# Feed-forward gate and up products by seven block products instead of eight, with the four weight sums of a pair on GpSimd

## The chip, the cores and the metric

One core of one Trainium2 chip. The time is the device time of one execution in microseconds (us), the median of several runs; lower is better.

## The reference, cut to what matters

The model has 528 tokens (16 learned and 512 given), a width of 1024 and two layers. The first layer mixes tokens by attention, the second by a recurrence (RWKV-7), and each ends in a feed-forward part. The change touches that part alone, and there the first of the two products:

```python
def swiglu(h, w_in, w_out):                      # w_in 1024 x 5632, w_out 2816 x 1024
    gate, up = jnp.split(jnp.einsum('btd,df->btf', h, w_in), 2, axis=-1)
    return jnp.einsum('btf,fd->btd', jax.nn.silu(gate) * up, w_out)

for i in range(DEPTH):
    ...
    h = h + mix
    h = h + swiglu(rms_norm(h, ffn_norm[i]), w_ffn_in[i], w_ffn_out[i])
return rms_norm(h[:, N_META:], final_norm)
```

## The kernel before, in words

Everything lies transposed: features on the 128 partitions, tokens along the row. A **unit** is a weight tile that gives 128 output features: 8 blocks of 128 x 128 (1024 inputs) for gate, up and the projections, 11 blocks for half of the 2816 hidden features. All weights are f32 in memory and are cut into two fp32r parts, high and low, so that each block needs three matmuls: high by high, high by low, low by high.

A unit goes through four engines, with two buffers of each kind. SyncE's DMA queue loads the raw tile (`load_unit`, L126). ScalarE copies it to fp32r (`w_hi`, L130). VectorE subtracts that from the raw tile (`w_lo`, L134). TensorE multiplies (`unit_products`, L790, and `Mlp.part`, L1257). The order on every engine is written out by hand, and semaphores hold them together.

The feed-forward part is the class `Mlp`. It first does 8 units of the mixer's output projection, each with the residual sum (L965), the high and low part of the normed input without its 1/rms (L893, L949) and the running sum of squares (L935); two small matmuls give the mean square (L1219) and ScalarE its inverse root by Ln and Exp (L900, L903). Then come, in each of two halves, 11 pairs of a gate and an up unit, and 8 output units that take the 11 hidden rows of the half. In the first layer the last 8 are cut in two by tokens, for the sake of the next stage. The first layer has 528 tokens, in two spans of 264, so a pair is 2 x 8 x 2 x 3 = 96 matmuls of 264 columns. The second layer works on the 512 given tokens in one span, so a pair is 48 matmuls of 512 columns.

Around a pair: VectorE multiplies the gate's result by 1/rms out of PSUM (L1013), ScalarE takes the sigmoid (L912), VectorE multiplies it in (L1017), does the same for up (L1023) and forms the product (L1029). ScalarE makes its high part `mid_hi` (L915) and GpSimd the low part `mid_lo` (L1181), but for the last row of a half, which VectorE does (L1033). These are the only operations of GpSimd in the two stages, apart from eight small `diag` tiles at the start of the second (L1176).

```python
for r in range(FHALF):                      # VectorE, one pair
    ...
    nc.vector.tensor_tensor(self.cols(b.gate), self.psum(0), self.cols(k.rstd), ALU.mult)
    self.lo(dve, g + 2)
    ...
    nc.vector.tensor_tensor(self.cols(b.up), self.psum(1), self.cols(k.rstd), ALU.mult)
```

Of the kernel before, what the change touches and what calls it, by code (L numbers as in the profile page):

```python
# [13 lines left out]
P = 128  # L14
# [780 lines left out]
MLP_UNITS = KT + 2 * (2 * FHALF + KT)  # L795
MLP_FIRST_UNITS = MLP_UNITS + KT


class Mlp:


    def __init__(self, k, n, wo, stages, nxt, first):
# [5 lines left out]
        self.gain = vcol(k, 'ffn_norm', n)  # L808
        self.srcs = [(wo.src(m // 2, m % 2), KT) for m in range(KT)]
        for half in range(2):  # L810
            g_in, g_out = stages[2 * half], stages[2 * half + 1]
            self.srcs += [(g_in.src(r, j), KT) for r in range(FHALF) for j in range(2)]
            for _ in range(2 if half and n == 0 else 1):
                self.srcs += [(g_out.src(m // 2, m % 2), FHALF) for m in range(KT)]
# [69 lines left out]
    def lo(self, dve, i):  # L884
        if self.split(i):
            unit_lo(self.k, dve, self.u0 + i, self.srcs[i][1])

    def scalar(self, act, b):
        k, nc = self.k, self.k.nc
        for m in range(KT):  # L890
# [7 lines left out]
            nc.scalar.activation(b.sq[m % 2][:, self.t0:T], k.res[:, m, self.t0:T], ACT.Square).then_inc(self.sq_r.h, 1)  # L898
        act.wait_ge(self.sum_r.h, 1)
# [3 lines left out]
        nc.scalar.activation(k.rstd[:, self.t0:T], k.rstd[:, self.t0:T], ACT.Exp, scale=-0.5).then_inc(self.rs_r.h, 1)  # L903
        for half in range(2):
            for r in range(FHALF):
                g, c = self.gate_unit(half, r), half * FHALF + r
                self.hi(act, g + 2)
                self.wait_freed(act, g)
                if c:

                    act.wait_ge(self.p_r.h, c)
                nc.scalar.activation(b.sig[:, self.t0:T], b.gate[:, self.t0:T], ACT.Sigmoid).then_inc(self.sg_r.h, 1)  # L912
                self.hi(act, g + 3)
                act.wait_ge(self.prod_r.h, c + 1)
                nc.scalar.activation(b.mid_hi[:, r, self.t0:T], b.up[:, self.t0:T], ACT.Copy).then_inc(self.mh_r.h, 1)  # L915
            if self.tail and half == 1:
                self.tail_scalar(act, b)
            elif half == 1:
                self.next_norm(act, b)
            else:  # L920
                for m in range(KT):
                    self.hi(act, self.out_unit(half, m) + 2)

    def vector(self, dve, b):
# [73 lines left out]
        for m in range(KT):  # L998
            residual(m, m)
            self.lo(dve, m + 2)  # L1000
            low(m)
            if m:
                accumulate(m - 1)
        accumulate(KT - 1)
        dve.wait_ge(self.rs_r.h, 2)
        for half in range(2):
            for r in range(FHALF):
                g, c = self.gate_unit(half, r), half * FHALF + r
                self.wait_done(dve, g)
                if c:  # L1010

                    dve.wait_ge(self.prod_r.h, c)
                nc.vector.tensor_tensor(self.cols(b.gate), self.psum(0), self.cols(k.rstd), ALU.mult)\  # L1013
                    .then_inc(self.freed(g), 1)
                self.lo(dve, g + 2)
                dve.wait_ge(self.sg_r.h, c + 1)
                nc.vector.tensor_tensor(b.gate[:, self.t0:T], b.gate[:, self.t0:T], b.sig[:, self.t0:T],  # L1017
                                        ALU.mult).then_inc(self.p_r.h, 1)
                self.wait_done(dve, g + 1)
                if c:  # L1020

                    dve.wait_ge(self.ml_r.h, c)
                nc.vector.tensor_tensor(self.cols(b.up), self.psum(1), self.cols(k.rstd), ALU.mult)\  # L1023
                    .then_inc(self.freed(g + 1), 1)
                if r < FHALF - 1:
                    self.lo(dve, g + 3)
                dve.wait_ge(self.p_r.h, c + 1)
                self.wait_freed(dve, g + 1)
                nc.vector.tensor_tensor(b.up[:, self.t0:T], b.up[:, self.t0:T], b.gate[:, self.t0:T],  # L1029
                                        ALU.mult).then_inc(self.prod_r.h, 1)  # L1030
                if r == FHALF - 1:
                    dve.wait_ge(self.mh_r.h, c + 1)
                    nc.vector.tensor_tensor(b.mid_lo[:, r, self.t0:T], b.up[:, self.t0:T],  # L1033
                                            b.mid_hi[:, r, self.t0:T].bitcast(F32), ALU.subtract).then_inc(self.ml_r.h, 1)
                    self.lo(dve, g + 3)
# [2061 lines left out]
```

## Time and profile before

| | us |
|---|---|
| runs | 1591.9, 1594.73, 1599.67 (median 1594.73) |
| span of the profiled execution | 1590.6 |
| TensorE busy with matmuls | 1530.2 (96%) |
| VectorE, ScalarE busy | 862.8 (54%), 645.3 (41%) |
| GpSimd busy | 163.6 (10%) |

The profile is of one execution. Its span runs from the first to the last instruction; the profile gives no other time for that execution, so what lies around the span isn't seen in it, and the median of the runs is 4.1 us above the span. Busy shares are averages over stages that differ; where a number below is of one stage, the stage's stretch is given in microseconds from the span's start. The first feed-forward lies at about 270 to 700, the second at about 1165 to 1580.

### The profile page before, as it was taken

The page shows a single profiled execution, that of the slowest core. Times are in us where ns is not written, and L with a number is a line of the kernel's source. Part 1 is how long each engine was busy: PE and PEld are TensorE (multiplying, and loading weights), DVE is VectorE, ACT ScalarE, POOL GpSimd, SP SyncE. Part 2 cuts the span into 40 slices and gives each one's busy share as a digit, 9 for nine tenths or more (in the row PEclk, how much of TensorE's full clock was granted, in tenths as well). Part 3 has the DMA queues.
Part 4 walks back from the last instruction along what each step waited for, and adds up shares of the span by engine and source line. Part 5 has one row for each costly group of instructions (what it writes and reads, how often), then busy time and mean ns, then how long its engine had stood idle before and what let it go on. Part 6 is the DMA issues. An engine that isn't in the chain of part 4 may idle for free. (4 is left out here: it accounts for less than half of the span.)

```text
span 1590.6 us, 33634 instructions
## 1 busy us (share of the span) xinstructions
PE 1530.2 (96%) x15009; PEld 1372.1 (86%) x15009; DVE 862.8 (54%) x1221; ACT 645.3 (41%) x896; POOL 163.6 (10%) x185
## 2 busy tenths in 40 slices
PE   7999998999999999998999999999889999999997
PEld 6988987999999999998998788888468888888886
DVE  5766765544432444587778655555765444344432
ACT  4654654332221222467588333333443232122222
POOL 3100100011100112400000410110010110001100
PEclk9999999999999999998999999999999999999999
DMA  4122122323332333563223100000323333233331
GB/s 136 55 60 74 55 66 54 105 81 93 103 92 78 88 93 108 151 181 134 81 66 91 54 3 4 4 5 4 108 59 93 100 93 110 76 93 94 104 104 56
DMA packets 226256, 127.62 MB, mean 80 GB/s; under 512 B 7960, under 2 KB 221104, under 8 KB 225856
## 3 DMA queue, kind: packets, MB, share of 16 engines
q1 hardware_dynamic: 225808, 125.39, 26.7%
q8 instruction: 119, 1.95, 0.5%
q14 instruction: 25, 0.20, 0.0%
q10 hardware_dynamic: 304, 0.08, 0.0%
HBM read 119.03 MB, written 6.42 MB: 79 GB/s over the span
## 5 line engine op out<-in xcount | busy, mean ns | idle before, releaser
L130 ACT ACTIVATE w_hi<-w_raw 128x1024 fp32r<-128x1024 f32 (+1 forms) x196 | 220.1, 1124 | 516.3 <-PE psg L790 307.4
L790 PE MATMUL psg<-x_hi,w_hi 128*128 128x264 f32 (+1 forms) x1080 | 350.9, 325 | 1.8 <-DVE w_lo L134 1.8
L790 PE MATMUL psg<-x_lo,w_hi 128*128 128x264 f32 (+1 forms) x1080 | 351.0, 325 | 0.0
L790 PE MATMUL psg<-x_hi,w_lo 128*128 128x264 f32 (+1 forms) x1080 | 350.2, 324 | 0.0
L134 DVE TENSOR_TENSOR w_lo<-w_raw,w_hi 128x1024 fp32r<-128x1024 f32 (+1 forms) x195 | 256.0, 1313 | 108.1 <-ACT w_hi L130 107.9
L790 PEld LDWEIGHTS psg<-x_hi,w_hi 128*128 128x128 f32 x1080 | 203.1, 188 | 20.2 <-DVE w_lo L134 2.2
L790 PEld LDWEIGHTS psg<-x_lo,w_hi 128*128 128x128 f32 x1080 | 203.2, 188 | 17.5 <-issue 0.2
L790 PEld LDWEIGHTS psg<-x_hi,w_lo 128*128 128x128 f32 x1080 | 203.7, 189 | 16.9
L1257 PE MATMUL psg<-mid_hi,w_hi 128*128 128x264 f32 (+1 forms) x528 | 170.8, 323 | 3.0 <-DVE w_lo L134 3.0
L1257 PE MATMUL psg<-mid_lo,w_hi 128*128 128x264 f32 (+1 forms) x528 | 170.0, 322 | 0.0
L1257 PE MATMUL psg<-mid_hi,w_lo 128*128 128x264 f32 (+1 forms) x528 | 169.4, 321 | 0.0
L1181 POOL TENSOR_TENSOR mid_lo<-up,mid_hi 128x528 fp32r<-128x528 f32 (+1 forms) x40 | 52.6, 1315 | 659.2 <-ACT mid_hi L915 659.2
L1257 PEld LDWEIGHTS psg<-mid_hi,w_hi 128*128 128x128 f32 x528 | 99.2, 188 | 12.1 <-DVE w_lo L134 4.1
L2070 PE MATMUL psg<-x_hi,w_hi 128*128 128x264 f32 (+1 forms) x320 | 100.6, 315 | 7.0 <-DVE w_lo L134 7.0
L1257 PEld LDWEIGHTS psg<-mid_lo,w_hi 128*128 128x128 f32 x528 | 99.2, 188 | 7.7
L1257 PEld LDWEIGHTS psg<-mid_hi,w_lo 128*128 128x128 f32 x528 | 99.3, 188 | 7.6
L965 DVE TENSOR_TENSOR res<-res,psg 128x512 f32<-128x512 f32 (+1 forms) x38 | 26.3, 693 | 145.1 <-PE psg L1257 116.9
L2070 PE MATMUL psg<-x_lo,w_hi 128*128 128x264 f32 (+1 forms) x320 | 99.6, 311 | 0.0
L2070 PE MATMUL psg<-x_hi,w_lo 128*128 128x264 f32 (+1 forms) x320 | 99.4, 311 | 0.0
L1013 DVE TENSOR_TENSOR gate<-psg,rstd 128x528 f32<-128x528 f32 (+1 forms) x44 | 30.8, 699 | 122.3 <-PE psg L790 115.3
L1023 DVE TENSOR_TENSOR up<-psg,rstd 128x528 f32<-128x528 f32 (+1 forms) x44 | 30.8, 700 | 112.4 <-PE psg L790 112.4
L2070 PEld LDWEIGHTS psg<-x_hi,w_hi 128*128 128x128 f32 x320 | 61.8, 193 | 11.4 <-DVE w_lo L134 8.1
(423 smaller groups left out, 3069.3 us busy)
## 6 DMA issues: line engine op xcount, KB each, us to landing
w_raw<-in_w_ffn_in_dram SPq DMA_DIRECT2D x88, 512.0 KB, 3.8
w_raw<-in_w_ffn_out_dram SPq DMA_DIRECT2D x40, 704.0 KB, 4.5
w_raw<-in_w_qkv_dram SPq DMA_DIRECT2D x24, 512.0 KB, 3.7
w_raw<-in_w_rkv_dram SPq DMA_DIRECT2D x24, 512.0 KB, 3.7
w_raw<-in_w_o_attn_dram SPq DMA_DIRECT2D x8, 512.0 KB, 3.6
w_raw<-in_w_o_rwkv_dram SPq DMA_DIRECT2D x8, 512.0 KB, 4.0
v_first<-v_pair SPq DMA_DIRECT2D x8, 264.0 KB, 2.0
kk_in<-v_first SPq DMA_DIRECT2D x1, 2112.0 KB, 10.7
```

The lines of the kernel that those rows point to most:

```text
L130: k.nc.scalar.activation(k.w_hi[j][:, 0:kt, :], k.raw[j][:, 0:kt, :], ACT.Copy).then_inc(k.hi_ready[j].h, 1)
L134: k.nc.vector.tensor_tensor(k.w_lo[j][:, 0:kt, :], k.raw[j][:, 0:kt, :], k.w_hi[j][:, 0:kt, :].bitcast(F32), ALU.subtract).then_inc(k.lo_r ...
L790: done = k.nc.tensor.matmul(k.psg[:, 2 * j + c, 0:size], w[:, t, :], x, start=t == first and n == 0, stop=t == last and n == 2)
L965: nc.vector.tensor_tensor(row, row, self.psum(i % 2), ALU.add).then_inc(self.freed(i), 1)
L1013: nc.vector.tensor_tensor(self.cols(b.gate), self.psum(0), self.cols(k.rstd), ALU.mult)\
L1023: nc.vector.tensor_tensor(self.cols(b.up), self.psum(1), self.cols(k.rstd), ALU.mult)\
L1181: nc.gpsimd.tensor_tensor(b.mid_lo[:, r, self.t0:T], b.up[:, self.t0:T], b.mid_hi[:, r, self.t0:T].bitcast(F32), ALU.subtract).then_inc(se ...
L1257: done = k.nc.tensor.matmul(self.bank(i, c), w[:, t, :], x, start=t == 0 and n == 0, stop=t == count - 1 and n == 2)
L2070: done = nc.tensor.matmul(k.psg[:, 2 * j + c, 0:size], w[:, t, :], x[:, at:at + size], start=t == 0 and a == 0, stop=t == KT - 1 and a == 2)
```

## The change

Of the 22 pairs of a layer the first two stay as they were. The other 20 are seen as a product of 2 x 2 blocks: the up and gate weights, each cut into its first and last 512 inputs (U0, U1, G0, G1), by the normed input, cut the same way and into two halves of the tokens (B11, B12, B21, B22; 264 or 256 tokens each). By Strassen's scheme in Winograd's form seven block products give what eight gave. It needs four sums of weights for every pair and four of inputs once a layer:

- `first_sum` S1 = G0 + G1, `second_sum` S2 = S1 - U0, `third_sum` S3 = U0 - G0, `fourth_sum` S4 = U1 - S2, each 128 x 512, all on GpSimd
- `input_sum` T1 = B12 - B11, T2 = B22 - T1, T4 = B21 - T2, T3 = B22 - B12, each 128 x 1056 (first layer) or 128 x 1024, on GpSimd as well
- products: one U0 B11, two U1 B21, three S4 B22, four G1 T4, five S1 T1, six S2 T2, seven S3 T3, each of 4 blocks x 3 = 12 matmuls of 264 or 256 columns (`pair_product`)

The parts that are multiplied are again cut into high and low: ScalarE makes the high parts (`high_up` 1024 columns, `high_gate` 512, `high_sums` twice 1024), VectorE the low ones (`low_up`, `low_gate`, `low_sums` of the same sizes). The low parts of the sums take the place of the sums. Three banks of PSUM hold the seven products of a pair. Product one, one plus six, and those plus seven are copied from bank 0 by ScalarE (`keep`, into spare rows); VectorE adds them to the other banks (`gate_late`, `up_early`, `up_late`), and gate's early half is read from bank 0 at the end (`sigmoid_early`, `gated_early`). The input is now multiplied by 1/rms before the products (`normalize`, eight times), so the readings from PSUM no longer are. There are two sets of weight buffers, x and y, used in turn.

The heart of the diff (`Mlp`; `wait_of(engine, signal, q)` waits for that signal of pair q, `wait_before` for that of the pair which last used the set):

```diff
+    def first_sum(self, pool, q):
+        p, gate = self.b.sets[pair_set(q)], self.raw_gate(q)
+        self.wait_gate(pool, q)
+        self.wait_before(pool, self.s.five, q)
+        self.k.nc.gpsimd.tensor_tensor(p.s[:, 0:KQ], gate[:, 0:KQ], gate[:, KQ:KT], ALU.add)
...
+    def high_sums(self, act, q, which):
...
+        self.wait_of(act, self.s.diff, q, 2, which + 1)
+        if which:
+            self.wait_of(act, self.s.sums, q, 2, 2)
+        self.wait_before(act, self.s.three if which else self.s.six, q)
...
     def gpsimd(self, pool, b):
...
+        for q in range(1, ALL_PAIRS):
+            if q not in (FIRST_PAIRS - 1, ALL_PAIRS - 1):
+                self.first_sum(pool, q + 1)
+                self.second_sum(pool, q + 1)
+                self.fourth_sum(pool, q + 1)
+                self.third_sum(pool, q + 1)
...
+            elif q != FIRST_PAIRS:
+                middle_low(q - 1 + PLAIN)
+        self.wait_of(pool, self.s.four, ALL_PAIRS - 1)
         if self.tail:
...
-        for half in range(2):
-            for r in range(FHALF - 1):
...
     def scalar(self, act, b):
...
+            for q in range(*((1, FIRST_PAIRS), (FIRST_PAIRS, ALL_PAIRS))[half]):
+                begun, last = q == FIRST_PAIRS, q in (FIRST_PAIRS - 1, ALL_PAIRS - 1)
+                if not begun:
+                    self.keep(act, q - 1, 2)
+                    self.sigmoid_late(act, q - 1)
+                self.keep(act, q, 0)
+                if not begun:
+                    self.high_gate(act, q)
+                if not last:
+                    self.high_up(act, q + 1)
+                    self.high_sums(act, q + 1, 0)
+                if not begun:
+                    self.sigmoid_early(act, q - 1)
...
+                    self.high_sums(act, q + 1, 1)
+                self.keep(act, q, 1)
+                if not begun:
+                    self.middle_high(act, q - 1 + PLAIN)
...
     def tensor(self, pe, b):
...
+            for q in range(*((0, FIRST_PAIRS), (FIRST_PAIRS, ALL_PAIRS))[half]):
+                begun = q in (0, FIRST_PAIRS)
+                self.product_one(pe, q)
+                self.product_five(pe, q)
+                if not begun:
+                    self.product_three(pe, q - 1)
+                    self.product_four(pe, q - 1)
+                self.product_six(pe, q)
+                self.product_two(pe, q)
+                self.product_seven(pe, q)
```

`product_seven` waits for the second `keep` of its pair and for the second `low_sums`; `product_five` for the first `low_sums`; `product_one` for `low_up` and for `gated_early` of two pairs before. SyncE loads the raw tiles of pair q once `low_up`, both `low_sums` and, for the gate tile, `low_gate` of pair q - 2 are done; the small loads of the next mixer come after those of the last pair, where before they came ahead of all units. Products three and four of the last pair of a half lie inside the first output unit.

On VectorE, a pair in the middle of the second layer was this before (`w_raw`, `w_hi`, `w_lo` are the weight buffers, `psg` is PSUM):

```order
L1013 TENSOR_TENSOR gate_15211<-psg,rstd 128x512 [waits m1_prod,unit_done0]
L134 TENSOR_TENSOR w_lo<-w_raw,w_hi 128x1024 [waits hi_ready0]
L1017 TENSOR_TENSOR gate_15211<-gate_15211,sig_15212 128x512 [waits m1_sig]
L1023 TENSOR_TENSOR up_15213<-psg,rstd 128x512 [waits m1_mid_lo,unit_done1]
L134 TENSOR_TENSOR w_lo<-w_raw,w_hi 128x1024 [waits hi_ready1]
L1029 TENSOR_TENSOR up_15213<-up_15213,gate_15211 128x512 [waits psum_free1,m1_act]
```

and is this now (in the order `gate_late`, `low_sums`, `gated_late`, `low_gate`, `up_late`, `low_sums` of the next pair, `gated_early`, `low_up` of the next pair, `product_row`, `up_early`; x and y are the two sets, `x_quarters` the spare rows):

```order
L1276 TENSOR_TENSOR gate_l_16053<-psx,x_quarters_l_16062 128x256 [waits m1_prod,a_sums_hi,a_z]
L1251 TENSOR_TENSOR y_sums_lo_l_16083<-y_sums_l_16082,y_sums_hi_l_16081 128x1024 [waits a_rest_hi]
L1282 TENSOR_TENSOR gate_l_16053<-gate_l_16053,sig_l_16054 128x256 [waits a_att]
L1242 TENSOR_TENSOR y_gate_lo_l_16080<-w_raw,y_gate_hi_l_16079 128x512 [waits a_ln]
L1303 TENSOR_TENSOR up_l_16055<-psx,x_quarters_l_16062 128x256 [waits a_first_turned]
L1251 TENSOR_TENSOR x_sums_lo_l_16074<-x_sums_l_16073,x_sums_hi_l_16072 128x1024 [waits a_summed,a_rest_hi]
L1288 TENSOR_TENSOR gate_l_16053<-psx,sig_l_16054 128x256 [waits a_att]
L1236 TENSOR_TENSOR x_up_lo_l_16069<-x_up_l_16075,x_up_hi_l_16068 128x1024 [waits a_exp]
L1311 TENSOR_TENSOR up_l_16055<-up_l_16055,gate_l_16053 128x512 [waits a_x_lo,a_sums_lo,a_half_read]
L1297 TENSOR_TENSOR up_l_16056<-psg,x_quarters_l_16062 128x256 [waits m1_mid_lo,a_sums_hi,a_half]
```

The two subtractions of 1024 columns have become three and one of 512, and the readings from PSUM are in halves of the tokens.

On GpSimd the second layer's loop was one row, twenty times:

```order
L1181 TENSOR_TENSOR mid_lo<-up_15213,mid_hi 128x512 [waits m1_mid_hi] x20
```

and a pair in the middle of the layer is this now (`first_sum`, `second_sum`, `fourth_sum`, `third_sum` of the next pair, then `mid_lo` of the previous pair):

```order
L1639 TENSOR_TENSOR x_sums_l_16073<-x_gate_l_16076 128x512 [waits a_z,a_x_late]
L1260 TENSOR_TENSOR x_sums_l_16073<-x_sums_l_16073,x_up_l_16075 128x512 [waits a_later,a_first_in,a_lo_near]
L1268 TENSOR_TENSOR x_sums_l_16073<-x_up_l_16075,x_sums_l_16073 128x512 [waits a_first_turned,a_summed]
L1646 TENSOR_TENSOR x_sums_l_16073<-x_up_l_16075,x_gate_l_16076 128x512 [waits a_v_turned,a_first_in]
L1662 TENSOR_TENSOR mid_lo_l_16061<-up_l_16056,mid_hi_l_16060 128x512 [waits m1_mid_hi]
```

`mid_lo` stands behind the sums of one pair and ahead of those of the next, and it waits for ScalarE's `mid_hi` of the previous pair.

## Rows read from the trace of the kernel before

**Rows 1.** The page: busy us, share of the span, instructions; GpSimd's busy tenths in 40 slices.
```profile
PE 1530.2 (96%) x15009; PEld 1372.1 (86%) x15009; DVE 862.8 (54%) x1221; ACT 645.3 (41%) x896; POOL 163.6 (10%) x185
...
POOL 3100100011100112400000410110010110001100
```

**Rows 2.** The chain of waits: start us, us, what; second feed-forward.
```profile
1204.96 5.57 PE psg L1257 x24
1210.52 0.86 PE psx L1219 x2
1211.38 116.78 PE psg L790 x504
```

**Rows 3.** Timeline of POOL (start us, us, instruction): mid_lo in the two layers.
```profile
328.77 1.32 POOL L1181 TENSOR_TENSOR mid_lo<-up,mid_hi 128x528 fp32r<-128x528 f32 x1 [73.00 <-ACT mid_hi L915]
...
433.95 1.33 POOL L1181 TENSOR_TENSOR mid_lo<-up,mid_hi 128x528 fp32r<-128x528 f32 x1 [10.37 <-ACT mid_hi L915]
...
1404.44 1.31 POOL L1181 TENSOR_TENSOR mid_lo<-up,mid_hi 128x512 fp32r<-128x512 f32 x1 [82.35 <-ACT mid_hi L915]
...
1415.56 1.29 POOL L1181 TENSOR_TENSOR mid_lo<-up,mid_hi 128x512 fp32r<-128x512 f32 x1 [9.81 <-ACT mid_hi L915]
```

**Rows 4.** Busy us of PE, PEld, DVE, ACT, POOL; granted clock, DMA share, GB/s.
```profile
320.00:440.00 120.00, 120.00 (x988) 120.00 (x987) 54.06 (x63) 36.68 (x44) 13.29 (x10) 1.00 0.32 92
```

**Rows 5.** Groups by shape: count | busy us, mean ns of one | idle before.
```profile
L134 DVE TENSOR_TENSOR w_lo<-w_raw,w_hi 128x1024 fp32r<-128x1024 f32 x43 | 52.7, 1226 | 19.6 <-ACT w_hi L130 19.6
...
L1029 DVE TENSOR_TENSOR up<-up,gate 128x512 f32<-128x512 f32 x22 | 15.1, 685 | 0.2
...
L130 ACT ACTIVATE w_hi<-w_raw 128x1024 fp32r<-128x1024 f32 x43 | 45.6, 1060 | 133.2 <-PE psg L790 120.3 <-PE psg L1257 12.9
...
L915 ACT ACTIVATE mid_hi<-up 128x512 fp32r<-128x512 f32 x22 | 13.9, 632 | 38.0 <-DVE up L1029 37.9
...
L1181 POOL TENSOR_TENSOR mid_lo<-up,mid_hi 128x528 fp32r<-128x528 f32 x20 | 26.6, 1330 | 346.1 <-ACT mid_hi L915 346.1
L1181 POOL TENSOR_TENSOR mid_lo<-up,mid_hi 128x512 fp32r<-128x512 f32 x20 | 26.0, 1300 | 313.1 <-ACT mid_hi L915 313.1
...
L2454 POOL TENSOR_TENSOR bk<-kk_in,w_inv 128x512 f32<-128x512 f32 x8 | 10.2, 1281 | 0.0
...
L1176 POOL TENSOR_SCALAR diag<-ident,vec 128x128 f32<-128x128 f32 x8 | 7.5, 958 | 66.9 <-DVE bonus L3017 66.9
```

**Rows 6.** Timeline of DVE and POOL near the kernel's start.
```profile
15.22 0.75 DVE L384 SCALAR_TENSOR_TENSOR x_lo<-res,vec,x_hi 128x528 fp32r<-128x528 f32 x1
15.89 2.33 DVE L134 TENSOR_TENSOR w_lo<-w_raw,w_hi 128x1024 fp32r<-128x1024 f32 x1
18.15 0.68 DVE L380 COPY res<-psx 128x512 f32<-128x512 f32 x1
18.75 1.22 DVE L384 SCALAR_TENSOR_TENSOR x_lo<-res,vec,x_hi 128x528 fp32r<-128x528 f32 x1
...
15.56 1.58 POOL L537 TENSOR_TENSOR x_acc<-x_acc,x_sq 128x528 f32<-128x528 f32 x1 [1.44 <-ACT x_sq L302]
...
17.29 2.11 POOL L537 TENSOR_TENSOR x_acc<-x_acc,x_sq 128x528 f32<-128x528 f32 x1
```

**Rows 7.** Timeline of DVE and POOL in the attention: DVE reads PSUM.
```profile
42.69 0.42 DVE L406 TENSOR_TENSOR v_pair<-psg,rstd 128x264 f32<-128x264 f32 x1
43.03 1.04 DVE L420 TENSOR_TENSOR rest<-rest,psg 128x864 f32<-128x864 f32 x1
...
43.56 1.31 POOL L543 TENSOR_TENSOR rest_lo<-rest,rest_hi 128x512 fp32r<-128x512 f32 x1 [18.49 <-ACT rest_hi L328]
```

**Rows 8.** Timeline of ACT after the row sum, second feed-forward.
```profile
1211.42 0.69 ACT L900 ACTIVATE rstd<-psx,eps 128x512 f32<-128x512 f32 x1 [4.17 <-PE psx L1219]
1212.14 0.63 ACT L903 ACTIVATE rstd<-rstd 128x512 f32<-128x512 f32 x1
```

**Rows 9.** DMA issues: KB each, median us from issue to landing.
```profile
w_raw<-in_w_ffn_in_dram SPq DMA_DIRECT2D x88, 512.0 KB, 3.8
```

More of the change, by code:

```diff
@@ L903, in scalar, with plain_sigmoid @@
         nc.scalar.activation(k.rstd[:, self.t0:T], k.rstd[:, self.t0:T], ACT.Exp, scale=-0.5).then_inc(self.rs_r.h, 1)
-        for half in range(2):
[L905 to L915, printed above, removed]
+        def plain_sigmoid(c):
+            self.wait_freed(act, self.plain_unit(c))
+            if c:
+                act.wait_ge(self.p_r.h, c)
+            nc.scalar.activation(b.sig[:, self.t0:T], b.gate[:, self.t0:T], ACT.Sigmoid).then_inc(self.sg_r.h, 1)
@@ L1003, in vector @@
                 accumulate(m - 1)
+            if m == 5:
+                self.low_sums(dve, 0, 0)
+            elif m == 6:
+                self.low_sums(dve, 0, 1)
+                self.low_gate(dve, 0)
         accumulate(KT - 1)
         dve.wait_ge(self.rs_r.h, 2)
-        for half in range(2):
[L1007 to L1035, printed above, removed]
@@ new lines, in vector @@
+        for m in range(KQ):
+            self.normalize(dve, m)
+        plain_gate(0)
+        self.lo(dve, self.plain_unit(1))
+        for m in range(KQ, KT):
+            self.normalize(dve, m)
+        plain_gated(0)
+        plain_up(0)
+        self.lo(dve, self.plain_unit(1) + 1)
+        self.low_up(dve, 0)
+        plain_product(0)
+        self.low_input(dve, 0)
+        plain_gate(1)
+        self.low_input(dve, 1)
+        plain_gated(1)
+        self.low_input(dve, 2)
+        plain_up(1)
@@ new lines, in vector @@
+        self.low_input(dve, 3)
+        plain_product(1)
+        self.low_input(dve, 4)
+        self.low_up(dve, 1)
+        self.low_sums(dve, 1, 0)
+        self.low_input(dve, 5)
+        self.low_input(dve, 6)
+        self.up_early(dve, 0)
+        for half in range(2):
+            for q in range(*((1, FIRST_PAIRS), (FIRST_PAIRS, ALL_PAIRS))[half]):
+                begun, last = q == FIRST_PAIRS, q in (FIRST_PAIRS - 1, ALL_PAIRS - 1)
+                if not begun:
+                    self.gate_late(dve, q - 1)
+                    self.low_sums(dve, q, 1)
+                    self.gated_late(dve, q - 1)
+                    self.low_gate(dve, q)
+                if not begun:
+                    self.up_late(dve, q - 1)
+                if not last:
+                    self.low_sums(dve, q + 1, 0)
+                if not begun:
+                    self.gated_early(dve, q - 1)
+                if not last:
+                    self.low_up(dve, q + 1)
+                if not begun:
+                    self.product_row(dve, q - 1)
+                if last:
+                    self.lo(dve, self.out_unit(half, 0))
+                self.up_early(dve, q)
+            self.gate_late(dve, q)
+            self.gated_late(dve, q)
+            self.up_late(dve, q)
+            self.lo(dve, self.out_unit(half, 1))
+            self.gated_early(dve, q)
+            self.product_row(dve, q)
+            c = q + PLAIN
+            dve.wait_ge(self.mh_r.h, c + 1)
+            dve.wait_ge(self.ml_r.h, c)
+            nc.vector.tensor_tensor(b.mid_lo[:, FHALF - 1, self.t0:T], b.up[c % 2][:, self.t0:T],
+                                    b.mid_hi[:, FHALF - 1, self.t0:T].bitcast(F32), ALU.subtract).then_inc(self.ml_r.h, 1)
@@ L1350, in build_program @@
         k.bodies += ATT_UNITS // 2
+        k.pair_signals = pair_signals(k, att)
         r = rwkv_arrays(k)
```

532 lines of the change are left out of this document (476 added, 56 removed).

## The prediction

> **What bounds the kernel now.** I read the page's busy shares first: PE is busy 96% of the span and POOL 10% [rows 1]. That alone would say: take matmuls away and give the extra work to POOL. The chain of waits confirms the first half. In the second feed-forward it holds nothing but PE: 504 matmuls of 512 columns in 116.78 us, with no wait inside [rows 2]. That is 231.7 ns for one, and 11.12 us for a pair of 48. POOL's next two starts there, 1404.44 and 1415.56, are the same 11.12 us apart [rows 3]. In the first feed-forward, from 328.77 to 433.95, POOL starts ten times; nine pairs in 105.18 us are 11.69 us each, or 121.8 ns for one of 96 matmuls of 264 columns [rows 3]. The stage table shows PE busy for all 120 us of that stretch, at full clock [rows 4]. So both stages run at PE's pace, and whatever VectorE, ScalarE and GpSimd do there is hidden, for now.
>
> Next come durations, from the groups kept apart by shape [rows 5]: a VectorE subtraction of 1024 columns takes 1.23 us and one of 512 0.69; ScalarE's copies take 1.06 and 0.63. GpSimd takes 1.30 for 512 columns into fp32r, 1.33 for 528, and 1.28 into plain f32. VectorE reads 264 columns of PSUM in 0.42 [rows 7].
>
> The view that decides is the timeline of the first 20 us, where VectorE and GpSimd both work on SBUF [rows 6]. GpSimd's sum starts at 15.56 while VectorE's x_lo runs, and takes 1.58, not 1.33, to 17.14. VectorE's w_lo begins at 15.89 and takes 2.33, not 1.23: it ends at 18.22, 1.08 after GpSimd. It goes the other way too: GpSimd's next sum, at 17.29, takes 2.11 and ends at 19.40, 1.18 after VectorE. The two never stream together; the second one starts its streaming when the first is done, and only some 0.15 us of set-up lies under the first. Against that, VectorE's 1.04 us operation at 43.03, with one input in PSUM, ran beside GpSimd's 1.31 us from 43.56 and neither grew [rows 7]. So the limit holds for VectorE with both inputs in SBUF. I call it **the shared port**.
>
> **PE's part.** Seven products of 12 matmuls replace 96 of 264 columns by 84. First layer: 12 x 0.1218 = 1.46 us saved a pair, 29.2 for 20. Second layer: 48 of 512 become 84 of 256. No row has 256 columns; between 264 (121.8) and 512 (231.7) the slope is 0.443 ns a column, so 118.2 ns by estimate, 9.93 us a pair, and 1.19 saved, 23.8 for 20. The bounds are 118.2 and 121.8, the latter for no gain from 8 fewer columns; I take the slope. PE's sum is -53.0 us.
>
> **The new work of a pair (second layer).** VectorE with both inputs in SBUF: low_up and two low_sums, 3 x 1.23; low_gate 0.69; one gating of 256 columns, 0.42 by the row of 264; the product row 0.69. Its four other operations, 0.42 each, have an input in PSUM and are free of the port. GpSimd: four weight sums at 1.28 and the mid_lo of 1.30. With 0.14 off each for the set-up, port time is 4.65 + 5.72 = 10.37 us, already above PE's 9.93. ScalarE has three of 1.06, two of 0.63 and five of about 0.42 (the slope between its two rows), 6.5 us in all, which hides.
>
> **The ring.** The programs are in order, so I walked one pair from a start to the same start one pair later. In this order each step waits for the one before: mid_hi on ScalarE 0.63 and 0.04 of hand-over; mid_lo 1.30 and 0.04; low_sums, second half, held by mid_lo, 1.09; first_sum, held by that, 1.14; gated_late 0.28; second_sum 1.14; low_gate 0.55; fourth_sum 1.14; third_sum straight behind it 1.23; low_sums of the next pair, first half, 1.09; gated_early 0.34; low_up 1.15; product_row 0.61, 0.04, and mid_hi again. The held ones are their duration less 0.14 (the rows give 1.23 less 1.08, 1.33 less 1.18, and 1.33 less the 1.17 from 15.22 + 0.75 to 17.14), VectorE's unheld ones less the 0.08 by which the next one overlaps (18.15 + 0.68 against 18.75 [rows 6]). The sum is **11.77 us** a pair, 1.84 above PE's 9.93 and 0.65 above the 11.12 of before. In the first layer five steps are 8 or 16 columns wider: 11.86, against 10.23 for PE's seven products and 11.69 before. PE feels it at seven(q): its keep of bank 0 stands on ScalarE behind high_sums, which waits for third_sum, which waits for the port. First_sum cannot be asked for earlier, since mid_lo stands ahead of it on POOL. Fifteen pairs a layer run so; the last of each half and the two at the turn have no four sums beside them and run at PE's pace, as does pair 0, which the start prices. The excess is 15 x 1.84 = +27.6 and 15 x 1.63 = +24.5.
>
> A page speaks against this change. The Trainium skill, "SBUF — State Buffer", in "SBUF: two separate sides", says that whichever of the two engines starts first gets the shared pair for its whole instruction while the other fully blocks, for VectorE operations with two SBUF inputs. That such operations exclude each other, the trace shows. That the hold lasts the whole instruction it does not show: some 0.15 us is covered in all three cases above. By that rule the time would be the third rival's 1657, and I go by the trace.
>
> **The start of each layer.** What must be there before product five of pair 1 can run: eight normalisings (0.75 less 0.08), five subtractions of 1024, five low_inputs of four quarters (about the same width) and four gatings, 5.4 + 5.45 + 5.45 + 2.2 = 18.5 on VectorE; four input sums of 1024 columns on GpSimd, two mid_lo and the sums of pairs 1 and in part 2. A GpSimd sum of 1024 appears nowhere; twice 1.28 less one set-up gives 2.4 less 0.14, 9.0 in all, with bounds of 8 and 10. The rest is 2.3 + 6.8. Together 36.7 us of port work in a row from the moment 1/rms is there. That is 7.3 us after the first gate unit starts: its 7/8 of 5.57, the row sum 0.86, then ScalarE's 0.69 and 0.63 [rows 2, 8]. So five(1) starts at 44.1. PE alone would be there after 2 x 11.12 + 0.86 + six products of 1.42 = 31.6: a wait of **12.5**. In the first layer the same is 44.8 against 33.0, **11.8**. Bounds: 0, if the port binds nothing, and 16, if set-up is not covered.
>
> **The ends.** After product four of the last pair: sigmoid, gating, product row, mid_hi and mid_lo take about 3.2 us, and PE has 2.8 us of the first output unit left in the second layer (0.4 wait, twice) and 1.4 us in the halved unit of the first (1.8 wait, once): 0.8 and 1.8. Bounds 0 and 3 each.
>
> **Costed at nothing.** Weight loads move the same 1 MB a pair, at 3.8 us from issue to landing for one [rows 9]; the raw gate of pair q+2 is asked for about 6.5 us into pair q and wanted 14 us in, a margin of 4. The small loads of the next mixer now go behind the last pair's on SP's queue; they have some 6 us of that pair as cover, and cost up to 3 if it is gone. The eight diag of the tail move on POOL behind product four of the last pair; they take 8 x 0.96 = 7.7 [rows 5], and the first transpose wants them two output units on, 11 us later.
>
> **Sum.** First layer -29.2 + 11.8 + 24.5 + 1.8 = +8.9. Second -23.8 + 12.5 + 27.6 + 0.8 = +17.1. Together **+26.0**. The profiled execution's span is 1590.6 and would be 1616.6; the runs shown have a median of 1594.7, 4.1 above it (within their own 1591.9 to 1599.7), so the time is **1621**, slower by 1.6%. A measurement here tells about 0.5%, 8 us, from nothing.
>
> **Rivals.**
> - *The port does not decide, and it gets faster.* Its place is the 30 ring pairs and the two starts. If GpSimd's sums and VectorE's subtractions mostly miss each other, fourth_sum and third_sum end 2.6 us after product three, high_sums and keep follow in 1.5, and seven(q) is due 4.3 after it: PE's pace is just met. Then -53.0 + 2.6 = 1544. It decides when the port is wanted for less than PE's 9.93 us. For: 40 mid_lo of before averaged 1.30 to 1.33, undisturbed [rows 5]. Against: [rows 6], and 10.37 above 9.93. Chance 0.07.
> - *The port binds but is never idle.* If stalls shift the order so that the 0.6 of mid_hi and the PSUM readings lie beside port work, a pair takes 10.37 (10.43 in the first layer). The excess falls to 15 x 0.44 and 15 x 0.20, and the sum is 1594.7 - 12.6 - 3.9 = 1578. For: in-order engines often fall into step. Against: mid_lo waits for mid_hi and blocks POOL. Chance 0.13, a part of it between this and no change.
> - *The hold lasts the whole instruction.* Seven hand-overs a pair cost 0.14 more, a pair is 12.75, 30 of them +29.4, the two starts +7.2: 1657. For: no row has this very pattern of hand-overs without a gap. Against: the three cases of [rows 6]. Late raw tiles or a lower granted clock in PE's waits would also lead there. Chance 0.15.
>
> **Chances.** The ring as walked has 0.65. Faster by over 0.5%: 0.07 and 0.09 of the second rival, 0.16. Within: the rest of that and a little of the ring, 0.08. Slower: 0.76. The range must leave out no more than 2 in 10: from 1582, which takes in most of the second rival's spread, to 1657. The ring's own range is 1608 to 1636: 12 us below and 15 above, by the bounds of starts and ends.
>
> **What would show it.** In the profile after: GpSimd's four sums longer than 1.28, many near 1.8 to 2.4, and low_sums and low_up well over 1.23, the sum of both engines' overshoot about 5 us a pair. Starts of the same sum 11.8 us apart in both layers. PE idle about 1.8 us a pair, released by ScalarE's keep or VectorE's lows, and 12 us in each start. It would be wrong if pairs come 10.2 and 9.9 us apart, if GpSimd's mean stays at 1.3, or if the wait ends with a DMA.

## The result and the profile after

| | before | after |
|---|---|---|
| median of the runs, us | 1595.99 | 1629.49 (1628.17 to 1632.52) |
| ratio | | 1.0215, 95% interval 1.0189 to 1.0241 |
| span of the profiled execution, us | 1590.6 | 1628.3 |

Slower by 2.1%, or 33.5 us, where 1.6% and 26 us had been forecast. The page's busy line and GpSimd's digits, which answer to [rows 1]:

```profile
PE 1496.5 (92%) x15489; PEld 1369.7 (84%) x15489; DVE 1104.7 (68%) x1411; ACT 757.5 (47%) x1150; POOL 452.0 (28%) x353
...
POOL 3100100166622664600000411010015563156510
```

TensorE lost 34 us of work, and the program became 38 us longer. Beside TensorE no engine is near full: VectorE shows 68%, GpSimd 28%. Busy shares alone would call this change safe. The view that tells more is the groups by shape (as [rows 5]: count | busy us, mean ns of one | idle before):

```profile
L1639 POOL TENSOR_TENSOR y_sums_l<-w_raw 128x512 f32<-128x512 f32 x18 | 40.4, 2247 | 104.0 <-DMA w_raw<-in_w_ffn_in_dram 104.0
L1268 POOL TENSOR_TENSOR y_sums_l<-w_raw,y_sums_l 128x512 f32<-128x512 f32 x18 | 31.4, 1742 | 1.4
...
L1251 DVE TENSOR_TENSOR x_sums_lo_l<-x_sums_l,x_sums_hi_l 128x1024 fp32r<-128x1024 f32 x44 | 86.3, 1965 | 17.4 <-POOL x_sums_l L1268 17.4
L1242 DVE TENSOR_TENSOR x_gate_lo_l<-x_gate_l,x_gate_hi_l 128x512 fp32r<-128x512 f32 x22 | 32.5, 1477 | 0.0
L1236 DVE TENSOR_TENSOR x_up_lo_l<-x_up_l,x_up_hi_l 128x1024 fp32r<-128x1024 f32 x20 | 24.2, 1209 | 0.0
L1282 DVE TENSOR_TENSOR gate_l<-gate_l,sig_l 128x256 f32<-128x256 f32 x20 | 23.7, 1185 | 1.0 <-ACT sig_l L1120 1.0
```

A first sum takes 2.25 us where GpSimd needs 1.28 for such an operation alone [rows 5]; VectorE's `low_sums` takes 1.97 instead of 1.23, `low_gate` 1.48 instead of 0.69, and a gating of 256 columns 1.19. `low_up` stays at 1.21: nothing of GpSimd's lies beside it in this order. How the lengths come about is seen in the timeline of one pair of the second layer (start us, us, instruction; VectorE first, then GpSimd):

```profile
1292.09 1.77 DVE L1251 TENSOR_TENSOR y_sums_lo_l<-y_sums_l,y_sums_hi_l 128x1024 fp32r<-128x1024 f32 x1
1293.78 1.51 DVE L1282 TENSOR_TENSOR gate_l<-gate_l,sig_l 128x256 f32<-128x256 f32 x1
1295.22 1.78 DVE L1242 TENSOR_TENSOR y_gate_lo_l<-w_raw,y_gate_hi_l 128x512 fp32r<-128x512 f32 x1
1296.92 0.41 DVE L1303 TENSOR_TENSOR up_l<-psx,x_quarters_l 128x256 f32<-128x256 f32 x1
1298.26 2.25 DVE L1251 TENSOR_TENSOR x_sums_lo_l<-x_sums_l,x_sums_hi_l 128x1024 fp32r<-128x1024 f32 x1 [0.93 <-POOL x_sums_l L1268]
...
1291.46 1.31 POOL L1662 TENSOR_TENSOR mid_lo_l<-up_l,mid_hi_l 128x512 fp32r<-128x512 f32 x1 [3.89 <-ACT mid_hi_l L1129]
1292.74 2.28 POOL L1639 TENSOR_TENSOR x_sums_l<-x_gate_l 128x512 f32<-128x512 f32 x1
1295.09 1.35 POOL L1260 TENSOR_TENSOR x_sums_l<-x_sums_l,x_up_l 128x512 f32<-128x512 f32 x1
1296.52 1.63 POOL L1268 TENSOR_TENSOR x_sums_l<-x_up_l,x_sums_l 128x512 f32<-128x512 f32 x1
1298.12 1.31 POOL L1646 TENSOR_TENSOR x_sums_l<-x_up_l,x_gate_l 128x512 f32<-128x512 f32 x1
```

Read the ends, start plus length. `mid_lo` ends at 1292.77; `low_sums`, begun before that, ends 1.09 later, at 1293.86; `first_sum`, begun at 1292.74, ends 1.16 after that, at 1295.02; the gating 0.27 later, 1295.29; `second_sum` 1.15, 1296.44; `low_gate` 0.56, 1297.00; `fourth_sum` 1.15, 1298.15; `third_sum` 1.28, 1299.43; `low_sums` 1.08, 1300.51. The two engines work in strict turns. That is the walk of the prediction, step for step, with `third_sum` 0.05 longer.

Two windows, each from one pair's first matmul after its wait to the next pair's, one in each layer (length, then busy us of PE, PEld, DVE, ACT, POOL), and TensorE's waits over the whole span (us in total, times, longest):

```profile
396.90:408.79 11.89, 10.46 (x84) 10.28 (x84) 10.27 (x11) 5.78 (x10) 7.79 (x5) 1.00 0.32 90
1300.98:1312.81 11.83, 10.10 (x85) 9.94 (x85) 10.21 (x11) 5.73 (x10) 7.77 (x5) 1.00 0.31 90
```
```profile
PE psx L1706 <- ACT x_quarters_l L1112: 36.1, 16, 7.1
PE psg L1706 <- ACT x_quarters_l L1112: 22.0, 14, 1.7
```

Back to back the 84 matmuls of a pair take 10.2 and 9.9 us (the runs below where nothing holds TensorE), and the pair lasts 11.89 and 11.83. The waits name ScalarE's `keep` (`x_quarters`, L1112): 30 of them, one of 7.1 us in each layer's start and 28 of 1.4 to 1.7 us, all ahead of product seven, of pairs 2 to 7 and 11 to 18 of each layer. ScalarE is busy for half the pair only; `keep` stands behind the high parts of the sums, which wait for GpSimd, which waits for the port. The engine named by a wait is the last link, not the cause.

**Where the time went.** From the first matmul of the first gate unit to the last of the last output unit the first layer's part grew from 392.7 to 403.1 us and the second's from 373.9 to 393.4, 29.9 us together. The rest of the 33.5 lies in the mixers and the start of the kernel, which move by that much from one profiled execution to another: over the kernel before and all the changed ones below, the first gate unit begins at 312.2 to 317.7 us, and between the two parts lie 496.6 to 507.6 us.

### The profile page after: what moved, and what is told of

Same layout as the page of the kernel before. It is cut to its first block and busy times, and to the rows that moved or that the text cites. A ratio compares the mean times of both kernels' runs of the same rounds, so it can differ in the third digit from the quotient of the medians.

```text
span 1628.3 us, 35699 instructions
## 1 busy us (share of the span) xinstructions
PE 1496.5 (92%) x15489; PEld 1369.7 (84%) x15489; DVE 1104.7 (68%) x1411; ACT 757.5 (47%) x1150; POOL 452.0 (28%) x353
## 5 line engine op out<-in xcount | busy, mean ns | idle before, releaser
L134 DVE TENSOR_TENSOR w_lo<-w_raw,w_hi 128x1024 fp32r<-128x1024 f32 (+1 forms) x115 | 167.5, 1457 | 67.1 <-ACT w_hi L130 66.5
L1863 PE MATMUL psg<-mid_hi_l,w_hi 128*128 128x264 f32 (+1 forms) x552 | 179.3, 325 | 4.1 <-DVE mid_lo_l L1492 2.2
L1863 PE MATMUL psg<-mid_lo_l,w_hi 128*128 128x264 f32 (+1 forms) x552 | 177.6, 322 | 0.0
L1863 PE MATMUL psg<-mid_hi_l,w_lo 128*128 128x264 f32 (+1 forms) x552 | 177.2, 321 | 0.0
L1863 PEld LDWEIGHTS psg<-mid_hi_l,w_hi 128*128 128x128 f32 x552 | 103.7, 188 | 14.2 <-DVE mid_lo_l L1492 3.2
L1863 PEld LDWEIGHTS psg<-mid_hi_l,w_lo 128*128 128x128 f32 x552 | 103.8, 188 | 8.0
L1863 PEld LDWEIGHTS psg<-mid_lo_l,w_hi 128*128 128x128 f32 x552 | 103.7, 188 | 7.9 <-issue 0.2
L2659 PE MATMUL psg<-x_hi,w_hi 128*128 128x264 f32 (+1 forms) x320 | 100.2, 313 | 7.9 <-DVE w_lo L134 7.9
L2659 PE MATMUL psg<-x_lo,w_hi 128*128 128x264 f32 (+1 forms) x320 | 99.3, 310 | 0.0
L2659 PE MATMUL psg<-x_hi,w_lo 128*128 128x264 f32 (+1 forms) x320 | 99.1, 310 | 0.0
L1251 DVE TENSOR_TENSOR x_sums_lo_l<-x_sums_l,x_sums_hi_l 128x1024 fp32r<-128x1024 f32 x44 | 86.3, 1965 | 17.4 <-POOL x_sums_l L1268 17.4
```

The source lines that it names most:

```text
L134: k.nc.vector.tensor_tensor(k.w_lo[j][:, 0:kt, :], k.raw[j][:, 0:kt, :], k.w_hi[j][:, 0:kt, :].bitcast(F32), ALU.subtract).then_inc(k.lo_r ...
L1251: self.k.nc.vector.tensor_tensor(p.s_lo[:, part], p.s[:, part], p.s_hi[:, part].bitcast(F32), ALU.subtract)\
L1863: done = k.nc.tensor.matmul(self.bank(i, c), w[:, t, :], x, start=t == 0 and n == 0, stop=t == count - 1 and n == 2)
L2659: done = nc.tensor.matmul(k.psg[:, 2 * j + c, 0:size], w[:, t, :], x[:, at:at + size], start=t == 0 and a == 0, stop=t == KT - 1 and a == 2)
```

## The experiments

Theory A is the prediction's: VectorE and GpSimd shut each other out while both read SBUF, and the order of the two programs turns that into a ring of 11.9 and 11.8 us. Pair lengths below are the distances of the same GpSimd instruction in successive pairs. Each run was measured beside new runs of the kernel before (their medians: 1596.6 for the run with the longer fills, 1594.1 for the last four in this section, 1595.7 for the others).

### Sums without reads

```diff
-        self.k.nc.gpsimd.tensor_tensor(p.s[:, 0:KQ], gate[:, 0:KQ], gate[:, KQ:KT], ALU.add).then_inc(self.s.sums.h, 1)
+        self.fill(p.s[:, 0:KQ]).then_inc(self.s.sums.h, 1)
```

and the same for the other three; `fill` is eight memsets of 128x64.

> Left out of the computation: the four weight sums of each of the 20 pairs; GpSimd writes zeros in their place (eight fills of 128x64 a sum, by the 0.145 us that such a fill takes in the profile some 1.16 us a sum, against 1.28 us for an undisturbed sum), with every wait and signal where it was. Everything else, the products' matmuls too, stays. Theory A (the ring: VectorE and GpSimd shut each other out while both read SBUF, and the two orders lock that into 11.9 and 11.8 us a pair): nothing reads SBUF beside VectorE, the pairs fall to TensorE's own pace, 10.2 us in layer 1 and 9.9 in layer 2, and the kernel to about 1563 us. Rival B (it is only GpSimd's distance and the chain of its waits, not the port): a sum is only 0.12 us shorter alone, so the pairs stay at 11.4 to 11.9 us and the kernel between 1610 and 1629 us. Third reading: fills take the port as well as reads do; then also 11.4 to 11.9 us, and VectorE's operations beside a fill would show it by their own stretched length.

Measured: 1567.91 us, ratio 0.9824 [0.98, 0.9847]; pairs 10.2 and 9.9 us. Theory A's numbers. But the fills came out too short:

```profile
1269.76 1.45 POOL L1637 MEMSET y_sums_l<- 128x64 f32 x16 [2.10 <-PE psg L1712]
```

Sixteen fills, two sums' worth, in 1.45 us. GpSimd's chain had shrunk by 2.1 us a pair, so rival B could have given the same. A second kernel put that right:

```diff
-            for c in (0, P // 2):
-                done = self.k.nc.gpsimd.memset(at[:, m, c:c + P // 2], 0.0)
+            for c in range(0, P, 32):
+                for w in range(c, c + 32, 16 if m < 2 and c < 96 else 32):
+                    done = self.k.nc.gpsimd.memset(at[:, m, w:w + (16 if m < 2 and c < 96 else 32)], 0.0)
```

> Left out of the computation: the four weight sums of each of the 20 pairs, as in the run with the fills. There the fills of 128x64 ran one behind the other at 0.09 us each, 0.75 us a sum where 1.16 was meant, so GpSimd's own chain was 2.1 us a pair shorter than with sums and that run couldn't tell the two theories apart. Here a sum is 22 fills (12 of 128x16, 10 of 128x32), by the slope between fills of 64 and of 512 columns about 1.2 to 1.3 us, the length of a sum alone. Theory A (the shared port): the same as with the shorter fills, 10.2 and 9.9 us a pair, 1563 to 1570 us. Rival B (GpSimd's distance and the chain of waits, without the port): 11.4 us a pair or more, 1610 us or more.

Measured: 1567.06 us, ratio 0.9817 [0.9781, 0.9853]; pairs 10.2 and 10.0 us. The timeline of GpSimd, and VectorE's groups of the run with the shorter fills:

```profile
1269.21 2.51 POOL L1638 MEMSET x_sums_l<- 128x16 f32 x44
1272.60 2.39 POOL L1638 MEMSET x_sums_l<- 128x16 f32 x44 [0.88 <-PE psx L1713]
```
```profile
L1251 DVE TENSOR_TENSOR x_sums_lo_l<-x_sums_l,x_sums_hi_l 128x1024 fp32r<-128x1024 f32 x44 | 53.5, 1220 | 9.8 <-POOL x_sums_l L1637 9.8
...
L1242 DVE TENSOR_TENSOR x_gate_lo_l<-x_gate_l,x_gate_hi_l 128x512 fp32r<-128x512 f32 x22 | 15.2, 691 | 0.2
```

44 fills, two sums, now take 2.4 to 2.5 us, 1.2 us a sum, close to a sum's own 1.28, with every wait in place. TensorE still sets the pace, and VectorE's operations are back at 1.22 and 0.69. Rival B falls: what costs is that GpSimd reads. (Fills write, and beside them VectorE isn't stretched.)

### Fewer matmuls

```diff
             for n, (w, x_part) in enumerate(((w_hi, x[0]), (w_hi, x[1]), (w_lo, x[0]))):
+                if n == 1 and t >= 2:
+                    continue
```

> Left out of the computation: in every block product the low-times-high term of two of four input blocks, 14 of a pair's 84 matmuls. Vector, scalar and GpSimd engines do what they did. Theory A (the ring sets the pairs): the pairs stay at 11.9 us (layer 1) and 11.8 us (layer 2) and TensorE waits 1.65 us a pair longer; the kernel stays within some 3 us of 1629. Rival C (TensorE, with its weight loads or a lowered clock, still sets the pace of the pairs, and the loss is elsewhere): 14 x 0.118 = 1.65 us less in each of 20 pairs of two layers, 66 us less, some 1563 us.

Measured: 1615.68 us, 13.8 less than the change, ratio 1.0128 [1.0089, 1.0167]. That misses both. The ring pairs did what A says: 11.9 and 11.8 us, and TensorE's waits for `keep` grew:

```profile
PE psx L1708 <- ACT x_quarters_l L1112: 57.9, 16, 7.4
PE psg L1708 <- ACT x_quarters_l L1112: 29.0, 18, 3.2
```

from 58.1 to 86.9 us. The 14 us came off outside the ring: the four halves of pairs, from first to last product, are 3.5 to 4.0 us shorter each, 14.7 in all. The expectation had forgotten the pairs that run at TensorE's pace. In the changed kernel 12 of the 40 do (0, 1, 8, 9, 10 and 19 of each layer), and 12 x 1.65 is 19.8; four of these, pairs 1 and 10, now wait 0.8 to 0.95 us each ahead of product seven, which takes 3.6 back. Of the remaining 1.5 us, 1.3 is a new wait ahead of product three of pair 0 in the first layer.

TensorE's waits grew by 28.8 us and not by 28 x 1.65 = 46, since the granted clock gave some of the saving back. In the first layer the ring's waits are 3.1 us and 1.7 us by turns. With each long one comes a stretch of 3.4 us with a granted clock of 0.50 (1.2 GHz, the lower of two levels; the first such at 379.63 to 383.04), TensorE's next products take longer, and the next wait is the short one. Two pairs together last 23.8 us as before. Rival C's 66 us is out.

### Two sums on VectorE

```diff
-        self.k.nc.gpsimd.tensor_tensor(p.s[:, KQ:2 * KQ], p.s[:, 0:KQ], self.raw_up(q)[:, 0:KQ], ALU.subtract)\
+        self.k.nc.vector.tensor_tensor(p.s[:, KQ:2 * KQ], p.s[:, 0:KQ], self.raw_up(q)[:, 0:KQ], ALU.subtract)\
```

and `fourth_sum` alike; on VectorE `second_sum(q + 1)` stands after `low_gate(q)`, `fourth_sum(q + 1)` before `low_sums(q + 1, 0)`.

> The second and the fourth sum go to VectorE, each in its place in the order; the first and third stay on GpSimd. The whole computation. Theory A: an undisturbed sum costs VectorE about as long as an operation of its own of the same tile (0.6 to 0.7 us) where it cost GpSimd 1.3 and waited for the other engine at every hand-over; the ring then works out at 11.35 us a pair in layer 1 and 11.27 in layer 2, 0.5 us less than now, and the kernel at about 1609 to 1614 us. Rival B (GpSimd's chain alone, without the port): two sums less on GpSimd take its chain out altogether, 10.2 and 9.9 us a pair, 1563 us or so. Rival D (VectorE is already full): two more sums on it make the pairs longer, by 1.3 us, over 13 us a pair and 1680 us.

Measured: 1608.9 us, ratio 1.008 [1.0055, 1.0105]; pairs 11.39 and 11.30 us. That is theory A to within 0.04 us a pair, and its 1609 to 1614 us to within 0.1. B and D both fall.

### The order alone

```diff
                     self.up_late(dve, q - 1)
-                if not last:
-                    self.low_sums(dve, q + 1, 0)
-                if not begun:
                     self.gated_early(dve, q - 1)
...
                 if last:
                     self.lo(dve, self.out_unit(half, 0))
+                else:
+                    self.low_sums(dve, q + 1, 0)
```

> One move on VectorE: the low parts of the next pair's first two sums are formed after the present pair's product row instead of before its late gate part. All four sums stay on GpSimd; nothing is added or left out. Theory A (the order of the ring, not the sum of the port's time, costs 1.4 of the 11.9 us): the ring closes at 10.62 us a pair in layer 1 and 10.56 in layer 2, against the 10.37 us that the two engines' reads take together, and the kernel falls to 1590 to 1596 us, about the kernel before the change. The second rival of the prediction (the port bound but never idle, 10.4 us a pair) put the whole change there: 1578 us. Rival E (the port's time itself is what has grown to 11.8 us a pair, so the order does not matter): pairs stay at 11.8, the kernel at 1629.

Measured: 1594.71 us, ratio 0.9993 [0.9975, 1.001]; pairs 10.84 and 10.63 us. One moved operation gives back 35 us, with no operation less. What VectorE does is the same, but the stretched operations are now others:

```profile
L1251 DVE TENSOR_TENSOR x_sums_lo_l<-x_sums_l,x_sums_hi_l 128x1024 fp32r<-128x1024 f32 x44 | 72.0, 1639 | 0.0
...
L1236 DVE TENSOR_TENSOR x_up_lo_l<-x_up_l,x_up_hi_l 128x1024 fp32r<-128x1024 f32 x20 | 34.5, 1724 | 0.0
```

Before the move VectorE stood idle for 17.4 us ahead of this `low_sums` group, waiting for `fourth_sum`; now it never does. The pairs are 0.22 and 0.07 us longer than theory A's walk gave (10.62 and 10.56), and why is open. They stop 0.41 us above the port's sum of 10.43 in the first layer and 0.26 above that of 10.37 in the second, so this order comes near what the port allows with all sums on GpSimd. Rival E falls.

### Three sums on VectorE

The move above, `second_sum` and `fourth_sum` on VectorE again, and `third_sum` with them, so that GpSimd keeps `first_sum` and `mid_lo`. `fourth_sum` and `third_sum` stand right behind `up_late`; ScalarE's `high_sums` waits for one counter of three a pair:

```diff
-        self.wait_of(act, self.s.diff, q, 2, which + 1)
-        if which:
-            self.wait_of(act, self.s.sums, q, 2, 2)
+        self.wait_of(act, self.s.diff, q, 3, 3 if which else 1)
```

> The move of the low parts, and the second, third and fourth sums on VectorE; GpSimd keeps the first sum and the middle's low part. The whole computation. Theory A (the two engines' reads add up, and a sum costs VectorE half of what it costs GpSimd): the ring is now shorter than TensorE's work, so the pairs come at TensorE's own pace, 10.2 us in layer 1 and 9.9 in layer 2, the kernel at 1575 to 1580 us, faster than the kernel before. Rival D (VectorE has no room for three more operations of 0.68 us in 10 us): pairs of 11 us or more, no faster than the run with the low parts' move alone, 1595 us.

Measured: 1575.35 us (1567.8 to 1582.97), ratio 0.9885 [0.9857, 0.9914]; pairs 10.20 and 9.94 us, TensorE's own pace; rival D falls. The six runs lie 15 us apart, and the profiled one was the slowest.

### The start too

```diff
-        self.k.nc.gpsimd.tensor_tensor(out, a, b, ALU.subtract).then_inc(s.t.h, 1)
+        self.k.nc.vector.tensor_tensor(out, a, b, ALU.subtract).then_inc(s.t.h, 1)
```

with `plain_gate(0)` and the low part of the next unit ahead of `normalize`, `input_sum` 0 after the fourth `normalize` and the other three after the first `low_input`.

> The same, and the four input sums at the start of each layer on VectorE as well, with the first plain gate part taken ahead of the normalised rows. The whole computation. Theory A (at the start a chain through GpSimd's 2.4 to 3.4 us input sums holds the first products back): the pairs as in the run with three sums on VectorE, and the first half's fifth product some 4 us earlier in each layer, together 7.5 us less than that run, 1567 to 1572 us. Rival F (the start waits for something else, the weights or the scaled quarters of VectorE's own row): no less than that run within 2 us.

Measured: 1565.58 us (1561.9 to 1569.53), ratio 0.9822 [0.98, 0.9844]. VectorE, groups by shape; a stretch of the first layer (as [rows 4]); TensorE's longest wait:

```profile
L1266 DVE TENSOR_TENSOR x_sums_l<-x_up_l,x_sums_l 128x512 f32<-128x512 f32 x20 | 13.6, 681 | 0.1
L1258 DVE TENSOR_TENSOR x_sums_l<-x_sums_l,x_up_l 128x512 f32<-128x512 f32 x20 | 13.6, 680 | 0.0
```
```profile
360.00:440.00 80.00, 80.00 (x660) 79.93 (x658) 68.21 (x98) 45.50 (x75) 21.34 (x15) 1.00 0.40 113
```
```profile
PE psx L1711 <- ACT x_quarters_l L1110: 14.4, 2, 7.3
```

A sum costs VectorE 0.68 us where GpSimd needs 1.28 and waits its turn besides. VectorE is now busy for 68 of 80 us, and TensorE for all 80. Of the 9.8 us between this median and the last one, 2 more than theory A gave, some 5 are seen in the two stages (3.5 us in each until product one of pair 0, of which 1.0 and 0.5 are lost again in the first half). The rest lies in stages whose code is the same in both, and so isn't this edit's: the trace of the run before has a granted clock of 0.50 there for 13.65 us from 1001.55 and again from 1056.17, and this one has not. What stays is a wait of 7.2 us in each layer's start, for `keep` of pair 0.

### All sums on VectorE, and the start alone

```diff
-        self.k.nc.gpsimd.tensor_tensor(p.s[:, 0:KQ], gate[:, 0:KQ], gate[:, KQ:KT], ALU.add).then_inc(self.s.sums.h, 1)
+        self.k.nc.vector.tensor_tensor(p.s[:, 0:KQ], gate[:, 0:KQ], gate[:, KQ:KT], ALU.add).then_inc(self.s.sums.h, 1)
```

> As the run before it, and the first sum on VectorE as well, so that GpSimd forms the middle's low part alone. The whole computation. Theory A: the pairs are already at TensorE's pace, so the ring has nothing to give; only the start, where the sums of pair 0 lie beside VectorE's work, could change, by under 2 us: 1565 to 1572 us, the same as the run before it. Rival D (VectorE full): pairs of over 10.5 us, 10 us or more slower than the run before it.

Measured: 1564.74 us, ratio 0.9822 [0.9798, 0.9845]; pairs 10.2 and 9.9: the same as the run before it. Once TensorE sets the pace, moving the last sum gives nothing.

The last one takes the start's edits alone onto the changed kernel.

> The changed kernel with its ring untouched (all four weight sums on GpSimd, the low parts where they were); only the four input sums are on VectorE and the first plain gate part ahead of the normalised rows. The whole computation. Theory A: pairs stay at 11.9 and 11.8 us; the starts of the two layers give 3.5 to 4 us each, 1617 to 1622 us against the changed kernel's 1629. Rival F: 1629 within 2 us.

Measured: 1621.27 us, 8.2 less than the change, ratio 1.0175 [1.0153, 1.0196]; pairs 11.91 and 11.84, as they were, and the two stages 4.1 and 3.2 us shorter. The start's path went through what these edits move, the input sums and the place of the first gate part, which weren't tried apart; rival F falls.

## Why the prediction was right, step by step

- **TensorE's part, -53.0.** Where nothing holds it, a pair takes 10.20 and 9.94 us (the runs with the fills and with the sums on VectorE) against the prediction's 10.23 and 9.93. The slope's estimate for 256 columns holds. The best kernels are still only 29 us faster than before, not 53, since the starts still cost: with the start's edits too, product five of pair 1 comes 45.4 and 44.2 us after the first gate unit, where TensorE alone would be there after 33.0 and 31.6.
- **The ring, +24.5 and +27.6.** Walked at 11.86 and 11.77 us, measured at 11.91 and 11.83. The prediction's steps as it lists them add up to 11.81, not 11.77, and `third_sum` directly behind `fourth_sum` takes 1.28 and not 1.23. Against that, TensorE waits ahead of product seven 14 times a layer, not 15: pair 1 was counted as a ring pair and runs within 0.2 us of TensorE's pace. Both are small. Beside the run with the start too, where TensorE sets the pace, the stretches from product five of pair 1 to product seven of pair 8 and from product one of pair 9 to product seven of pair 19 are 24.2 us longer in the first layer and 27.0 in the second. The fills show the cause, and the move of `low_sums` shows that 1.1 to 1.2 us of each pair is the order's.
- **The starts, +11.8 and +12.5.** This term was too small, and part of its way was another. Product five of pair 1 came 48.1 and 47.1 us after the first gate unit's first matmul (317.65 to 365.76, 1222.92 to 1270.01), forecast 44.8 and 44.1; by the same sum that is +15.1 and +15.5. The row of port work ended about where it was put: the first `low_sums` of pair 1 was done after 44.1 and 43.1 us. But product five did not wait for it. TensorE's long wait, 7.1 us, came four products earlier, ahead of product six of pair 0, for `keep`, which stood on ScalarE behind a `mid_hi` that waited for VectorE's product row. And behind that wait TensorE was slow. The stretch of products six, two and seven of pair 0, in each layer (as [rows 4]):

```profile
357.20:364.30 7.10, 7.10 (x36) 7.10 (x37) 7.10 (x5) 3.14 (x4) 5.62 (x3) 0.58 0.00 0
1261.52:1268.58 7.06, 7.06 (x36) 7.06 (x37) 7.06 (x5) 3.07 (x4) 5.56 (x3) 0.57 0.00 0
```

  The granted clock had fallen to 0.50 (1.2 GHz) while TensorE waited and rose again in the third of the three products. They took 7.1 us each time, where the prediction's 1.46 and 1.42 a product give 4.4 and 4.3: 2.7 and 2.8 us lost. The sum has every product at full clock; a lower clock is named only beside the third rival. At full clock product five would have come after 45.4 and 44.3 us, close to the forecast, but behind another wait than the one forecast, so the closeness is in part luck. The input sums, taken as 2.4 us from two GpSimd operations of 512, are that when undisturbed:

```profile
1233.07 2.40 POOL L1655 TENSOR_TENSOR t_sums_l<-x_quarters_l 128x1024 f32<-128x1024 f32 x1 [29.44 <-DVE x_quarters_l L1321]
1239.28 6.13 POOL L1655 TENSOR_TENSOR t_sums_l<-x_quarters_l,t_sums_l 128x1024 f32<-128x1024 f32 x2 [3.81 <-DVE x_quarters_l L1321]
1245.36 3.37 POOL L1655 TENSOR_TENSOR t_sums_l<-x_quarters_l 128x1024 f32<-128x1024 f32 x1
```

  Beside VectorE they take 3 us and more, as the row of port work in the prediction has it. The 3.81 us before the second was no port work, though, but a wait for `normalize`; that the start is one unbroken row was a simplification, and the row's end came 0.7 and 1.0 us before its forecast.
- **The ends, +1.8 and +0.8.** TensorE waited 2.2 us in all, three times, for the last `mid_lo` of a half; what is left of the two stages' growth after the other terms is 1.5 us.
- **The sum, +26.0.** The two stages grew by 10.4 and 19.5 where 8.9 and 17.1 were forecast, 3.9 us more together. The starts cost 6.3 more than forecast, of which 5.5 is the lower clock; the ring cost 0.9 less, TensorE's part saved 0.4 more, and the ends cost 1.1 less. The other 3.6 us of the medians' difference lie in unchanged code. The 1629.5 stands 8.5 above the forecast 1621, also because the median of the kernel before is 1596.0 with a fourth run, where the prediction had 1594.7.
- **The signs.** Pairs, GpSimd's sums, `low_sums` and the waits for `keep` came as described. `low_up` was to be well over 1.23 us and stayed at 1.21; the prediction's own walk has it beside no GpSimd operation.
- **The rivals.** "The port does not decide" is what the fills made true for the ring, and they gave 1567, not 1544. They left the input sums on GpSimd, and even with those on VectorE the kernel stays at 1565: the rival's sum had nothing for the starts, where TensorE keeps waiting for `keep` (3.5 us a layer with fills, 7.2 with the sums on VectorE). "The port binds but is never idle" is what the moved line made nearly true: 1594.7 against its 1578, with pairs 0.41 and 0.26 us longer than it said, and with starts that cost 6 us more than the 24.3 it had for them. "The hold lasts the whole instruction" is out: it gave pairs of 12.75 us, and the hand-overs of the timeline above take 1.09, 1.16 and 1.15 us, for operations of 1.23 and 1.28. Here case and the Trainium skill, "SBUF — State Buffer", "SBUF: two separate sides", part in size only: the exclusion is as it says, and it sets the changed kernel's time, but 0.12 to 0.15 us of each held operation costs nothing, since it lies beside the operation that holds it up. Which part of the operation that is, these records don't show.

## What to carry to other kernels

GpSimd's idle time isn't free when VectorE works from SBUF: add up what both want from SBUF per round of the loop. Here a sum moved to the "idle" engine cost nearly twice what it costs VectorE (1.28 against 0.68 us), and 10.4 us of such time stood against 9.9 us of TensorE work. Above that, walk the ring: with the same operations, the place of one subtraction decided 35 us. And where a stage begins with a wait of TensorE, look at the granted clock behind it: a sum at full clock missed 2.7 and 2.8 us in the two starts. The kernel with three of the four sums on VectorE, one `low_sums` moved and the input sums on VectorE as well runs in 1565.6 us, 1.8% under the kernel before (interval 1.6 to 2.0) and 3.9% under the change.

## What was not expected of the hardware

- Small GpSimd fills overlap: one of 128x64 lasts 0.15 us by its record, and sixteen in a row take 1.45 us, 0.09 each. Lengths of single short instructions can't be added up.
- GpSimd's fills, which only write, stretched no VectorE operation (1.22 us beside them, as alone). Only reads were seen to shut the other engine out.
- A VectorE gating of 256 or 264 columns, 0.41 us alone, took 1.50 to 1.53 us each of the 28 times that it fell behind GpSimd's `first_sum`: the hand-over costs the other engine's whole remainder, however short one's own work is.
- In every run a wait of TensorE in a layer's start (3.4 to 8.3 us) was followed by products at the lower of the two clock levels, in the runs with fills and in the fastest kernels as well: in the run with the start too the clock was at 0.50 for 10.24 us from 345.73 and for 6.83 us from 1222.95.
